# Alternating row halves and column halves of TensorE in the attention stage of a one-layer decoder kernel

## The chip, the cores and the metric

The kernel runs on one core of a Trainium2 chip. The metric is the device time of one execution in microseconds (us); lower is better. All data are f32.

## The reference, cut to what matters

One decoder layer over 256 tokens of width 1024: an RMS norm, a combined input projection, two attention branches beside each other, gates and output projection, and then a sparse feed-forward layer with 32 experts, of which each token takes four. The two branches are what matters here:

```python
# branch A (MLA): 8 heads, keys and queries of 64 + 32 = 96, values of 64, one K and V per head
s = (einsum('bqhd,bkhd->bhqk', qn, k_nope) + einsum('bqhr,bkr->bhqk', qp, k_rot)) * 96 ** -0.5
p = softmax(where(causal, s, -inf));  out_a = einsum('bhqk,bkhd->bqhd', p, v)

# branch B (DSA): an indexer picks 64 keys per query, then 8 query heads share ONE K and ONE V of 64
rel = relu(einsum('bqhd,bkd->bqhk', q_idx, k_idx) * 64 ** -0.5)      # 8 index heads, one index key
score = where(causal, einsum('bqh,bqhk->bqk', w_idx, rel), -inf)
_, sel = top_k(score, 64)
s = einsum('bqhd,bqkd->bhqk', q, k[sel]) * 64 ** -0.5
p = softmax(where(valid, s, -inf));      out_b = einsum('bhqk,bqkd->bqhd', p, v[sel])
```

The kernel doesn't gather: it computes all scores of branch B and adds a mask of the keys that aren't selected.

## The kernel before, in words

Every engine runs its own program, written out by hand, and waits on counting semaphores. There is no planner: the order of the text is the order of each engine's queue. The 256 tokens are two tiles of 128 (`t` = 0, 1). Because of causality a query tile `t` needs only `w = 128 * (t + 1)` keys.

**Front stage.** `raw` is a ring of six slots of 2 MB into which SP (`load_front`, L410) loads the weights in order. `z_unit` (L516) does the input projection in four parts. The index queries are turned (`turn_pairs`, L544) into `qT`, which holds two heads per column block: the even head in rows 0 to 63 and the odd head in rows 64 to 127. `kT` holds the one key twice, in both row halves. Then come the index scores (L589), the turning of branch B's queries, the up projections of branch A (L616), the turning of its queries and keys (L634), and the attention loop (L681). `gate_block` (L558) is a piece of other work, 16 of which compute the gates; the tables `GATES_IDX` and `GATES_ATT` (L61, L62) say after which batches one is put in, to give PE something to do while other engines work. One block is eight matmuls of 256 columns. Then come the branch projections (`branch`, L690), the output projection, and the router.

**Batches.** Heads are worked on in batches that fill one PSUM bank of 512 columns: `BATCHES` (L54) has six for one branch, two for `t` = 0 with four heads and four for `t` = 1 with two heads. All heads of one batch have the same parity, so they lie in the same row half of `qT`. In PSUM, head `h`'s output of a value product goes to partitions `64 * (h % 2)` and on, so all value products of one batch lie in the same column half of the array.

`scores` (L531) writes batch `b` to bank `SB[b % 2]`. In the index stage ACT applies a ReLU from there to `prob` (L954, signal `idx_rl`), and DVE adds the weighted heads up into `score` (L1188, L1190, signal `idx_ac`). ACT's ReLU `b` waits for DVE's sum of batch `b - 2`; PE's batch `b` waits for ReLU `b - 2`.

**Attention loop** (L681), 12 batches, 0 to 5 of branch A and 6 to 11 of branch B. Round `b` on PE: `scores_of(b + 1)`, `values(b - 1)`, a gate block, `turn_probs(b)`. The score products of branch A have 96 rows, those of branch B have 64. DVE's `masked(b)` (L1252) scales and masks the scores and takes the maximum, ACT's `exps` (L992) exponentiates, DVE's `normalised(b)` (L1274, signal `p_ok`) divides; PE's `turn_probs(b)` (L654) waits for `p_ok` and transposes; ACT copies the result to `probT` (L1018, signal `pT_ok`), for which `values(b)` (L662) waits. `masked(b)` waits until `turn_probs(b - 2)` has read the same buffer (`pT_ps`). Between these, DVE works off the top-k selection of branch B (`topk`, L1201) in pieces of three rounds, and the rest of it ahead of `masked(6)`.

```python
            for b in range(12):
                if b < 11:
                    scores_of(b + 1)
                if b:
                    values(b - 1)
                if b in GATES_ATT:
                    gate_block()
                turn_probs(b)
```

**Expert loop** (L885). Per item four `gate_up` and two `down` units of 2 MB each go through the ring; PE, per unit, adds one to `used` and SP loads the next unit into the freed slot (L473). The expert loads before that, the first of them while the front stage still runs, wait for the front units whose slots they take (`used_up`, L348).

In the profile, lines are those of the innermost helper: L493 is `gemm` (gate blocks, up projections, `branch`), L497 a transpose, L535 a score product, L672 a value product, L770 the gather of tokens, L803 the scatter, L835 `gate_up`.

Of the kernel before, what the change touches and what calls it, by code (L numbers as in the profile page):

```python
# [8 lines left out]
ACT = mybir.ActivationFunctionType  # L9
# [5 lines left out]
P = 128  # L15
# [8 lines left out]
Q_LORA, KV_LORA, NOPE, ROPE, V_DIM = 256, 128, 64, 32, 64  # L24
QK = NOPE + ROPE
HD, ROT = 64, 16
# [24 lines left out]

BATCHES = [(0, (0, 2, 4, 6)), (0, (1, 3, 5, 7)),  # L54
           (1, (0, 2)), (1, (1, 3)), (1, (4, 6)), (1, (5, 7))]


WARM = (4, 10, 6, 4)


GATES_IDX = (3,)  # L61
GATES_ATT = (0, 1, 2, 3, 4, 5, 6, 7, 8, 9, 10)  # L62


# [20 lines left out]
def build(nc, x, positions, attn_norm_g, w_in, mla_q_norm_g, mla_w_uq, mla_kv_norm_g, mla_w_ukv,  # L85
# [4 lines left out]
    with ctx:  # L90
# [42 lines left out]
        v_ml = fb("v_ml", [P, TT, HEADS, V_DIM])  # L133
# [61 lines left out]
        B = [ctx.enter_context(nc.psum_tensor(f"bank{i}", [P, BLK], F32)) for i in range(8)]  # L195
        ZB, TB, SB, VB = B[0:2], B[2:4], B[4:6], B[6:8]
        TURN = TB + SB
        ACC, GU, PREP, DN = B[0:4], B[4:6], B[6], B[7]

        def const(name, rows=P):  # L200
# [289 lines left out]
        def _(pe):  # L490
# [5 lines left out]
            def turned(o, src):  # L496
                return pe.transpose(o, src, ident)  # L497
# [30 lines left out]
                    mm.then_inc(z_ps, 1)  # L528
                    z_n += 1

            def scores(b, q, k, signal):  # L531
                t, heads = BATCHES[b % 6]
                w = P * (t + 1)
                for m, h in enumerate(heads):
                    mm = pe.matmul(SB[b % 2][:, m * w:(m + 1) * w], q(h, t), k(h, w), start=True, stop=True)  # L535
                mm.then_inc(signal, 1)

            def pair_q(h, t):
                return qT[HD * (h % 2):HD * (h % 2) + HD, h // 2, t * P:(t + 1) * P]

            def pair_k(h, w):
                return kT[HD * (h % 2):HD * (h % 2) + HD, 0:w]

            def turn_pairs(zq, signal):  # L544

                for j in range(4):
                    for t in range(TT):
                        a = (j % 2) * TOKENS + t * P
                        tr = turned(TB[j // 2][:, a:a + P], zq[:, t, j * P:(j + 1) * P])
                    if j % 2:  # L550
                        tr.then_inc(signal, 1)
                for t in range(TT):
                    tr = turned(VB[0][:, t * P:(t + 1) * P], kk[:, t, :, :].rearrange("p a d -> p (a d)"))
                tr.then_inc(signal, 1)
# [31 lines left out]
            turn_pairs(z_qi, qi_ps)  # L586
            z_unit(3)
            pe.wait_ge(qi_ok, 3)
            for b in range(6):  # L589
                if b >= 2:  # L590
                    pe.wait_ge(idx_rl, b - 1)
                scores(b, pair_q, pair_k, idx_ps)
                if b in GATES_IDX:
                    gate_block()

            pe.wait_ge(qb_rot, 1)
            turn_pairs(z_qb, qd_ps)
            gate_block()

# [46 lines left out]
            def scores_of(b):  # L646
                if b >= 2:
                    pe.wait_ge(s_mx, b - 1)
                if b < 6:
                    scores(b, lambda h, t: qmT[:, h, t * P:(t + 1) * P], lambda h, w: kmT[:, h, 0:w], s_ps)  # L650
                else:
                    scores(b, pair_q, pair_k, s_ps)

            def turn_probs(b):  # L654
                pe.wait_ge(p_ok, b + 1)
                if b >= 2:
                    pe.wait_ge(pT_ok, b - 1)
                for m in range(4):
                    tr = turned(TB[b % 2][:, m * P:(m + 1) * P], prob[:, b % 2, m * P:(m + 1) * P])
                tr.then_inc(pT_ps, 1)  # L660

            def values(b):  # L662
                t, heads = BATCHES[b % 6]
                pe.wait_ge(pT_ok, b + 1)
                if b in (6, 8):
                    pe.wait_ge(pv_ok, t + 1)
                for m in range(4):
                    h = heads[m // (t + 1)]
                    kt = m % (t + 1)
                    half = V_DIM * (h % 2)  # L670
                    v = v_ml[:, kt, h, :] if b < 6 else z_kv[:, kt, HD:2 * HD]
                    mm = pe.matmul(VB[t][half:half + V_DIM, (h // 2) * P:(h // 2 + 1) * P], v,  # L672
                                   probT[:, b % 2, m * P:(m + 1) * P], start=kt == 0, stop=kt == t)
                mm.then_inc(pv_ps, 1)

# [3 lines left out]
            pe.wait_ge(up_a, 8)  # L679
            scores_of(0)  # L680
            for b in range(12):  # L681
                if b < 11:
                    scores_of(b + 1)
                if b:
                    values(b - 1)
                if b in GATES_ATT:
                    gate_block()
                turn_probs(b)
# [8 lines left out]
            pe.wait_ge(pv_ok, 2)  # L697
            pe.wait_ge(s_mx, 12)
            branch(0, 0)
            values(11)  # L700
            branch(0, 1)
            landed_front(pe, U_BR + 1)
            pe.wait_ge(pv_ok, 4)
# [204 lines left out]
        def _(act):  # L908
# [41 lines left out]
            for b in range(6):  # L950
                act.wait_ge(idx_ps, b + 1)
                if b >= 2:
                    act.wait_ge(idx_ac, b - 1)
                act.activation(prob[:, b % 2, :], SB[b % 2][:, :], ACT.Relu, scale=HD ** -0.5).then_inc(idx_rl, 1)  # L954
                if b in GATES_IDX:
                    gate_evac()
            for j in range(2):
                act.wait_ge(qd_ps, j + 1)
# [31 lines left out]
                act.copy(qmT[:, 2 * j:2 * j + 2, :].rearrange("p h t -> p (h t)"), TURN[2 * j % 4][0:QK, :]).then_inc(mq_ok, 1)  # L990

            def exps(b):  # L992
                t, heads = BATCHES[b % 6]
                w = P * (t + 1)
                act.wait_ge(s_mx, b + 1)
                for m in range(len(heads)):
                    ex = act.activation(prob[:, b % 2, m * w:(m + 1) * w], prob[:, b % 2, m * w:(m + 1) * w], ACT.Exp,
                                        bias=mx[:, b % 2, m:m + 1], accum_out=den[:, b % 2, m:m + 1])
                ex.then_inc(p_ex, 1)
# [110 lines left out]
        def _(dve):  # L1110
# [68 lines left out]
            dve.tensor_tensor(rw[:, :, :], rw[:, :, :], g_ffn[:, :].unsqueeze(2).to_broadcast([P, KC, EXPERTS]),  # L1179
                              ALU.mult).then_inc(rw_ok, 1)  # L1180
            for b in range(6):
                t, heads = BATCHES[b]
# [12 lines left out]
                dve.wait_ge(idx_ac, b + 1)  # L1195
# [55 lines left out]

            def masked(b):  # L1252

                t, heads = BATCHES[b % 6]
                w, n = P * (t + 1), len(heads)
                scale = (QK if b < 6 else HD) ** -0.5
                src = SB[b % 2][:, :].rearrange("p (h k) -> p h k", h=n)
                pr = prob[:, b % 2, :].rearrange("p (h k) -> p h k", h=n)
                dve.wait_ge(s_ps, b + 1)
                if b >= 2:  # L1260
                    dve.wait_ge(pT_ps, b - 1)
                if b >= 6:
                    mask = allow[:, t, 0:w].unsqueeze(1).to_broadcast([P, n, w])
                    step(dve.scalar_tensor_tensor(out=pr, in0=src, scalar=scale, in1=mask, op0=ALU.mult, op1=ALU.add))
                else:
                    if t:
                        dve.tensor_scalar(pr[:, :, 0:P], src[:, :, 0:P], scale, None, ALU.mult)
                    mask = const("causal").unsqueeze(1).to_broadcast([P, n, P])
                    step(dve.scalar_tensor_tensor(out=pr[:, :, t * P:w], in0=src[:, :, t * P:w], scalar=scale, in1=mask,
                                                  op0=ALU.mult, op1=ALU.add))  # L1270
                step(dve.tensor_reduce(mx[:, b % 2, 0:n], pr, AXX, ALU.max))
                dve.tensor_scalar(mx[:, b % 2, 0:n], mx[:, b % 2, 0:n], -1.0, None, ALU.mult).then_inc(s_mx, 1)

            def normalised(b):  # L1274
                t, heads = BATCHES[b % 6]
# [243 lines left out]
```

## Time and profile before

| | |
|---|---|
| median of 3 runs | 1183.23 us (1181.96 to 1184.37) |
| the profiled execution | 1181.82 us, span 1180.0 us |
| mean granted TensorE clock | 0.995 |
| PE (matmul) busy | 1102.3 us, 93% |
| PE weight loads | 473.9 us, 40% |
| DVE busy | 279.0 us, 24% |
| ACT busy | 164.0 us, 14% |
| POOL busy | 10.2 us, 1% |
| read from memory | 429.92 MB, 365 GB/s over the span |

The span is what the trace covers, from the first instruction to the last; the execution's own time is 1.82 us longer. Busy shares are averages over stages that differ: the front stage, some 240 us, and the expert loop, the rest. A record `64*128 64x256 f32 x8` is eight records of matmuls that use 64 rows and 128 columns of the array and stream 256 columns of data; a matmul of f32 leaves two records, a transpose one. The records of a matmul are pipelined, so a group's duration overlaps with the start of the next one.

### The profile page before, as it was taken

How to read it: one execution, taken by the hardware profiler on the slowest of the kernel's cores; microseconds unless marked ns; L12 is line 12 of the kernel's file. 1: busy time of each engine (PE TensorE's matmuls, PEld its weight loads, DVE VectorE, ACT ScalarE, POOL GpSimd, SP SyncE). 2: the span in 40 equal slices, each digit the busy share in tenths (PEclk: the TensorE clock that was granted, in tenths of full speed). 3: DMA queues.
4: the chain of work that ended last, by engine and by line, in shares of the span. 5: the costliest groups of instructions: out<-in, count | busy, mean ns of one | idle time of the engine just before them, and what ended most of it. 6: DMA issues, size and time to landing. Idle time of an engine off the chain costs nothing.

```text
span 1180.0 us, 13249 instructions
## 1 busy us (share of the span) xinstructions
PE 1102.3 (93%) x5094; PEld 473.9 (40%) x5094; DVE 279.0 (24%) x662; ACT 164.0 (14%) x341; POOL 10.2 (1%) x28
## 2 busy tenths in 40 slices
PE   7999999999999999999999999999999999999996
PEld 5578887633333333333333333333333333333332
DVE  2056432321111211111111111111111111111113
ACT  2144440210001000000000000000000000000002
POOL 0101000000000000000000000000000000000000
PEclk9999999999999999999999999999999999999998
DMA  9823313469999999999999999999999999999993
GB/s 307 315 75 147 136 72 126 160 288 405 429 429 430 427 427 430 429 428 427 429 429 429 427 427 430 429 428 427 429 429 430 427 427 430 429 428 427 429 429 158
DMA packets 43265, 431.22 MB, mean 365 GB/s; under 512 B 5808, under 2 KB 7984, under 8 KB 18640
## 3 DMA queue, kind: packets, MB, share of 16 engines
q1 hardware_dynamic: 42960, 430.46, 87.2%
q10 hardware_dynamic: 288, 0.52, 0.1%
q8 instruction: 11, 0.18, 0.1%
q14 instruction: 6, 0.05, 0.0%
HBM read 429.92 MB, written 1.05 MB: 365 GB/s over the span
## 4 chain that ended last, share of the span: by engine, by line
DMA 57%; PE 41%; DVE 1%; issue 1%; ACT 1%; SPq 0%; DVEq 0%; ACTq 0%
DMA raw<-in_w_gate_up 56%; PE bank L835 15%; PE bank L493 8%; PE bank L526 4%; PE bank L851 4%; PE bank L718 2%; PE bank L497 2%; PE bank L535 1%; PE bank L672 1%; PE bank L770 1%; PE bank L803 1%; DMA x_res<-in_x 1%; PE bank L736 0%; PE bank L813 0%; DVE x_res L1457 0%
## 5 line engine op out<-in xcount | busy, mean ns | idle before, releaser
L835 PE MATMUL bank<-raw,xT 128*64 128x512 f32 x2048 | 465.2, 598 | 56.0 <-DMA raw<-in_w_gate_up 54.4
L835 PEld LDWEIGHTS bank<-raw,xT 128*64 128x64 f32 x2048 | 137.9, 136 | 357.7 <-issue 230.7
L851 PE MATMUL bank<-raw,actT 128*64 128x512 f32 x1024 | 233.2, 597 | 0.0
L1408 DVE COPY ev_gu<-bank 128x512 f32<-128x512 f32 x32 | 22.1, 692 | 532.7 <-PE bank L835 532.7
L851 PEld LDWEIGHTS bank<-raw,actT 128*64 128x64 f32 x1024 | 71.7, 137 | 132.5 <-issue 126.7
L1401 DVE TENSOR_TENSOR gub<-bank,bias_gu 128x512 f32<-128x512 f32 x64 | 43.9, 686 | 169.5 <-PE bank L497 169.5
L1065 ACT COPY ev_gu<-bank 128x512 f32<-128x512 f32 x32 | 18.8, 586 | 413.3 <-PE bank L835 413.3
L803 PE MATMUL bank<-ev_dn,scat 64*128 64x512 f32 x256 | 64.3, 621 | 1.2 <-ACT ev_dn L1075 0.8
L770 PE MATMUL bank<-x_res,onehot 128*64 128x512 f32 x264 | 62.3, 592 | 0.0
L493 PE MATMUL bank<-hT,raw 128*128 128x256 f32 x256 | 58.9, 383 | 0.0
L493 PEld LDWEIGHTS bank<-hT,raw 128*128 128x128 f32 x256 | 47.5, 190 | 8.4 <-issue 2.5
L526 PE MATMUL bank<-raw,hT 128*128 128x512 f32 (+2 forms) x128 | 46.4, 525 | 1.1 <-DVE hT L1142 1.1
L497 PEld LDWEIGHTS bank<-cst,ev_gu 128*128 128x128 f32 x256 | 33.4, 211 | 25.9 <-issue 25.9
L1070 ACT ACTIVATE sig<-gub 128x512 f32<-128x512 f32 x32 | 20.1, 629 | 154.7 <-DVE gub L1410 154.7
L497 PE MATMUL bank<-cst,ev_gu 128*128 128x128 f32 x256 | 39.5, 297 | 0.0
L803 PEld LDWEIGHTS bank<-ev_dn,scat 64*128 64x128 f32 x256 | 22.1, 186 | 41.7 <-issue 41.0
L770 PEld LDWEIGHTS bank<-x_res,onehot 128*64 128x64 f32 x264 | 19.0, 137 | 37.2 <-issue 37.0
L526 PEld LDWEIGHTS bank<-raw,hT 128*128 128x128 f32 x128 | 25.1, 202 | 20.5 <-issue 20.4
L1075 ACT COPY ev_dn<-bank 128x512 f32<-128x512 f32 x32 | 18.8, 586 | 83.1 <-PE bank L851 83.1
L1060 ACT COPY scat<-bank 128x256 f32<-128x256 f32 x32 | 11.9, 372 | 126.7 <-PE bank L497 126.7
L1051 ACT COPY ev_x<-bank 128x512 f32<-128x512 f32 x33 | 19.3, 586 | 66.5 <-PE bank L770 66.5
L1424 DVE TENSOR_TENSOR actT<-gub,sig 128x512 f32<-128x512 f32 x32 | 22.2, 692 | 24.5 <-PE bank L851 24.5
(234 smaller groups left out, 594.1 us busy)
## 6 DMA issues: line engine op xcount, KB each, us to landing
raw<-in_w_gate_up SPq DMA_DIRECT2D x128, 2048.0 KB, 25.4
raw<-in_w_down SPq DMA_DIRECT2D x64, 2048.0 KB, 24.9
raw<-in_w_in SPq DMA_DIRECT2D x6, 2048.0 KB, 14.5
raw<-in_w_out SPq DMA_DIRECT2D x2, 2048.0 KB, 9.7
raw<-in_w_branch_mla SPq DMA_DIRECT2D x1, 2048.0 KB, 9.0
raw<-in_w_branch_dsa SPq DMA_DIRECT2D x1, 2048.0 KB, 7.8
raw<-in_w_in SPq DMA_DIRECT2D x1, 1664.0 KB, 16.8
x_res<-in_x SPq DMA_DIRECT2D x2, 512.0 KB, 4.9
```

Source lines behind the costliest of these rows:

```text
L493: mm = pe.matmul(o, lhs(c), rhs(c), start=start and c == 0, stop=c == n - 1)
L497: return pe.transpose(o, src, ident)
L526: mm = pe.matmul(ZB[t][:, 0:w], hT[:, c, t * P:(t + 1) * P], unit3(n, w)[:, c, :], start=c == 0, stop=c == KC - 1)
L718: mm = pe.matmul(B[2 * t + n][:, :], mT[:, c, t * P:(t + 1) * P], unit3(U_WO + n)[:, c, :], start=c == 0, stop=c == KC - 1)
L770: mm = pe.matmul(PREP[half * SLOTS:(half + 1) * SLOTS, :], onehot[:, t, :], xs[:, t, half * BLK:(half + 1) * BLK], start=t == 0, stop=t == ...
L803: mm = pe.matmul(ACC[2 * t + half][:, :], scat[rows, t * P:(t + 1) * P], ev_dn[rows, :], start=False, stop=True, skip_group_check=True)
L835: mm = pe.matmul(GU[pair][half * SLOTS:(half + 1) * SLOTS, :], xT[:, c, b, :], w[:, at:at + BLK], start=u == 0 and k == 0, stop=last and k ...
L851: mm = pe.matmul(DN[half * SLOTS:(half + 1) * SLOTS, :], actT[:, c, u, :], w[:, at:at + BLK], start=u == 0 and c == 0, stop=u == DN_UNITS ...
L1070: act.activation(sig[:, :], glu, ACT.Sigmoid, scale=ALPHA).then_inc(sig2_ok, 1)
L1401: dve.tensor_tensor(gub[:, pair, :].rearrange("p (j s) -> p j s", s=SLOTS), GU[pair][:, :].rearrange("p (j s) -> p j s", s=SLOTS), bias_gu ...
L1408: dve.tensor_copy(ev_gu[:, 1, :], GU[1][:, :]).then_inc(lin_ev, 1)
L1424: dve.tensor_tensor(actT[:, :, :, :].rearrange("p c h s -> p (c h s)"), lin, sig[:, :], ALU.mult).then_inc(act_ok, 1)
```

## The change

The score products with 64 rows (index scores and branch B's scores) are issued in pairs of batches, the even head in the upper and the odd head in the lower rows in turn, each into its own bank. `PAIR_BATCHES` is the old table. The index scores use `SB`, `TB` and `SB` again, and their gate block comes after batches 2 and 3. Branch A's batches hold neighbouring heads now, so that its 64-wide value products alternate between the column halves; their order is by key tile first. Branch B's value products have the same V for all heads, so each half's product streams all heads of the batch at once (512 columns for `t` = 0, 256 for `t` = 1), and `turn_probs` puts the transposed blocks in that order for `b >= 8`. In the loop, branch B's scores come at `b` = 5, 7 and 9, its value products at `b` = 8 and 10 and after the loop.

```diff
-BATCHES = [(0, (0, 2, 4, 6)), (0, (1, 3, 5, 7)),
-           (1, (0, 2)), (1, (1, 3)), (1, (4, 6)), (1, (5, 7))]
+BATCHES = [(0, (0, 1, 2, 3)), (0, (4, 5, 6, 7)),
+           (1, (0, 1)), (1, (2, 3)), (1, (4, 5)), (1, (6, 7))]
+PAIR_BATCHES = [(0, (0, 2, 4, 6)), (0, (1, 3, 5, 7)),
+                (1, (0, 2)), (1, (1, 3)), (1, (4, 6)), (1, (5, 7))]
-GATES_IDX = (3,)
+GATES_IDX = (2,)
+        IDX_BANKS = (SB, TB, SB)
...
+            def pair_scores(b, banks, signal):
+                t = PAIR_BATCHES[b][0]
+                w, n = P * (t + 1), len(PAIR_BATCHES[b][1])
+                for m in range(n):
+                    for k in range(2):
+                        h = PAIR_BATCHES[b + k][1][m]
+                        rows = slice(HD * k, HD * k + HD)
+                        mm = pe.matmul(banks[k][:, m * w:(m + 1) * w], qT[rows, h // 2, t * P:(t + 1) * P], kT[rows, 0:w],
+                                       start=True, stop=True)
+                        if m == n - 1:
+                            mm.then_inc(signal, 1)
...
-            for b in range(6):
-                if b >= 2:
-                    pe.wait_ge(idx_rl, b - 1)
-                scores(b, pair_q, pair_k, idx_ps)
+            for b in range(0, 6, 2):
+                if b == 4:
+                    pe.wait_ge(idx_rl, 2)
+                pair_scores(b, IDX_BANKS[b // 2], idx_ps)
                 if b in GATES_IDX:
                     gate_block()
             pe.wait_ge(qb_rot, 1)
+            pe.wait_ge(idx_rl, 4)
             turn_pairs(z_qb, qd_ps)
...
                 if b < 6:
-                    scores(b, lambda h, t: qmT[:, h, t * P:(t + 1) * P], lambda h, w: kmT[:, h, 0:w], s_ps)
+                    scores(b)
                 else:
-                    scores(b, pair_q, pair_k, s_ps)
+                    pe.wait_ge(s_mx, b)
+                    pair_scores(b - 6, SB, s_ps)
...
-                    tr = turned(TB[b % 2][:, m * P:(m + 1) * P], prob[:, b % 2, m * P:(m + 1) * P])
+                    at = (m % 2) * 2 + m // 2 if b >= 8 else m
+                    tr = turned(TB[b % 2][:, at * P:(at + 1) * P], prob[:, b % 2, m * P:(m + 1) * P])
...
             def values(b):
-                t, heads = BATCHES[b % 6]
+                t, heads = BATCHES[b]
                 pe.wait_ge(pT_ok, b + 1)
-                if b in (6, 8):
-                    pe.wait_ge(pv_ok, t + 1)
-                for m in range(4):
-                    h = heads[m // (t + 1)]
-                    kt = m % (t + 1)
-                    half = V_DIM * (h % 2)
-                    v = v_ml[:, kt, h, :] if b < 6 else z_kv[:, kt, HD:2 * HD]
-                    mm = pe.matmul(VB[t][half:half + V_DIM, (h // 2) * P:(h // 2 + 1) * P], v,
-                                   probT[:, b % 2, m * P:(m + 1) * P], start=kt == 0, stop=kt == t)
+                for kt in range(t + 1):
+                    for n, h in enumerate(heads):
+                        m = n * (t + 1) + kt
+                        half = V_DIM * (h % 2)
+                        mm = pe.matmul(VB[t][half:half + V_DIM, (h // 2) * P:(h // 2 + 1) * P], v_ml[:, kt, h, :],
+                                       probT[:, b % 2, m * P:(m + 1) * P], start=kt == 0, stop=kt == t)
                 mm.then_inc(pv_ps, 1)
+            def pair_values(b):
+                t, heads = PAIR_BATCHES[b - 6]
+                pe.wait_ge(pT_ok, b + 2)
+                pe.wait_ge(pv_ok, t + 1)
+                n = len(heads) * P
+                at = (heads[0] // 2) * P
+                for kt in range(t + 1):
+                    for k in range(2):
+                        mm = pe.matmul(VB[t][V_DIM * k:V_DIM * (k + 1), at:at + n], z_kv[:, kt, HD:2 * HD],
+                                       probT[:, (b + k) % 2, kt * n:(kt + 1) * n], start=kt == 0, stop=kt == t)
+                        if kt == t:
+                            mm.then_inc(pv_ps, 1)
...
             for b in range(12):
-                if b < 11:
+                if b < 6 or b in (7, 9):
                     scores_of(b + 1)
-                if b:
+                if 0 < b < 7:
                     values(b - 1)
+                elif b in (8, 10):
+                    pair_values(b - 2)
                 if b in GATES_ATT:
                     gate_block()
                 turn_probs(b)
...
             branch(0, 0)
-            values(11)
+            pair_values(10)
             branch(0, 1)
```

ACT's ReLU reads from `IDX_BANKS` and evacuates the index stage's gate block after batch 3; ACT's and DVE's loops take their heads from the table that PE uses. Their instructions are the same in number and size.

## Rows read from the trace of the kernel before

**Rows 1.** The page's 40 equal slices (29.5 us each): PE busy, granted clock, memory rate.

```profile
PE   7999999999999999999999999999999999999996
PEclk9999999999999999999999999999999999999998
GB/s 307 315 75 147 136 72 126 160 288 405 429 429 430 427 427 430 429 428 427 429 429 429 427 427 430 429 428 427 429 429 430 427 427 430 429 428 427 429 429 158
```

**Rows 2.** Timeline of the SP queue, 0 to 250 us: start, length, what.

```profile
140.19 107.54 SPq L435 DMA_DIRECT2D raw<-in_w_gate_up  x8
```

**Rows 3.** Timeline of PE at the index scores (second row: a window of the first part).

```profile
61.32 3.52 PE L535 MATMUL bank<-kT,qT 64*128 64x128 f32 x24
...
61.32 1.71 PE L535 MATMUL bank<-kT,qT 64*128 64x128 f32 x16
...
64.77 3.72 PE L493 MATMUL bank<-hT,raw 128*128 128x256 f32 x16
68.42 1.14 PE L535 MATMUL bank<-kT,qT 64*128 64x256 f32 x8
69.50 1.09 PE L497 MATMUL bank<-cst,z_qb 128*128 128x128 f32 x8
```

**Rows 4.** The chain that ended last, at the index scores: start, length, what.

```profile
62.51 0.60 ACT area_p L954
...
63.16 1.68 PE bank L535 x8
```

**Rows 5.** Timeline of PE in the attention loop, b=6 (first two rows) and b=7.

```profile
134.34 1.16 PE L535 MATMUL bank<-kT,qT 64*128 64x128 f32 x8
135.42 1.09 PE L672 MATMUL bank<-area_p,v_ml 128*64 128x128 f32 x8
...
140.00 0.60 PE L497 MATMUL bank<-cst,area_p 128*128 128x128 f32 x4
140.53 1.13 PE L535 MATMUL bank<-kT,qT 64*128 64x256 f32 x4
141.58 1.09 PE L672 MATMUL bank<-area_p,z_kv 128*64 128x128 f32 x8
142.60 3.72 PE L493 MATMUL bank<-hT,raw 128*128 128x256 f32 x16
146.16 0.60 PE L497 MATMUL bank<-cst,area_p 128*128 128x128 f32 x4
```

**Rows 6.** Timeline of PE around one gather (L770) and one scatter (L803).

```profile
254.06 1.89 PE L770 MATMUL bank<-x_res,onehot 128*64 128x512 f32 x8
255.88 0.69 PE L813 MATMUL bank<-gain,gateT 32*128 32x512 f32 x1
...
294.39 1.99 PE L803 MATMUL bank<-ev_dn,scat 64*128 64x512 f32 x8
296.31 1.08 PE L835 MATMUL bank<-raw,xT 128*64 128x512 f32 x4
```

**Rows 7.** Timeline of PE: the transposes of `turn_probs(2)` and `turn_probs(3)`.

```profile
115.67 0.60 PE L497 MATMUL bank<-cst,area_p 128*128 128x128 f32 x4
...
121.65 0.60 PE L497 MATMUL bank<-cst,area_p 128*128 128x128 f32 x4
```

**Rows 8.** Timeline of DVE: the last instruction of `normalised(2)` and `normalised(3)`.

```profile
113.60 0.69 DVE L1280 TENSOR_TENSOR area_p<-area_p,den 128x512 f32<-128x512 f32 x1
...
120.62 0.69 DVE L1280 TENSOR_TENSOR area_p<-area_p,den 128x512 f32<-128x512 f32 x1
```

**Rows 9.** Busy us (instructions) in a stretch: PE, weight loads, DVE, ACT, POOL; clock, DMA.

```profile
112.00:118.00 6.00, 6.00 (x34) 4.95 (x32) 5.69 (x17) 2.52 (x7) 0.00 (x0) 1.00 0.13 34
```

**Rows 10.** Timeline of PE from `turn_probs(10)` to the branch projection; in brackets idle time.

```profile
164.65 0.60 PE L497 MATMUL bank<-cst,area_p 128*128 128x128 f32 x4
165.92 1.09 PE L672 MATMUL bank<-area_p,z_kv 128*64 128x128 f32 x8 [0.68 <-ACT area_p L1018]
...
170.27 1.99 PE L493 MATMUL bank<-q_ml,raw 128*128 128x256 f32 x8
```

More of the change, by code:

```diff
@@ L529, in z_unit, with scores @@
                     z_n += 1
-            def scores(b, q, k, signal):
-                t, heads = BATCHES[b % 6]
+            def scores(b):
+                t, heads = BATCHES[b]
                 w = P * (t + 1)
                 for m, h in enumerate(heads):
[L535 to L542, printed above, removed]
+                    mm = pe.matmul(SB[b % 2][:, m * w:(m + 1) * w], qmT[:, h, t * P:(t + 1) * P], kmT[:, h, 0:w],
+                                   start=True, stop=True)
+                mm.then_inc(s_ps, 1)
+            def pair_scores(b, banks, signal):
[6 more added lines that the diff above has]
+                        mm = pe.matmul(banks[k][:, m * w:(m + 1) * w], qT[rows, h // 2, t * P:(t + 1) * P], kT[rows, 0:w],
+                                       start=True, stop=True)
+                        if m == n - 1:
+                            mm.then_inc(signal, 1)
             def turn_pairs(zq, signal):
@@ L658, in turn_probs @@
                 for m in range(4):
-                    tr = turned(TB[b % 2][:, m * P:(m + 1) * P], prob[:, b % 2, m * P:(m + 1) * P])
+                    at = (m % 2) * 2 + m // 2 if b >= 8 else m
+                    tr = turned(TB[b % 2][:, at * P:(at + 1) * P], prob[:, b % 2, m * P:(m + 1) * P])
                 tr.then_inc(pT_ps, 1)
             def values(b):
-                t, heads = BATCHES[b % 6]
+                t, heads = BATCHES[b]
                 pe.wait_ge(pT_ok, b + 1)
-                if b in (6, 8):
-                    pe.wait_ge(pv_ok, t + 1)
-                for m in range(4):
-                    h = heads[m // (t + 1)]
-                    kt = m % (t + 1)
-                    half = V_DIM * (h % 2)
-                    v = v_ml[:, kt, h, :] if b < 6 else z_kv[:, kt, HD:2 * HD]
-                    mm = pe.matmul(VB[t][half:half + V_DIM, (h // 2) * P:(h // 2 + 1) * P], v,
-                                   probT[:, b % 2, m * P:(m + 1) * P], start=kt == 0, stop=kt == t)
-                mm.then_inc(pv_ps, 1)
+                for kt in range(t + 1):
[4 more added lines that the diff above has]
+                                       probT[:, b % 2, m * P:(m + 1) * P], start=kt == 0, stop=kt == t)
+                mm.then_inc(pv_ps, 1)
+            def pair_values(b):
[10 more added lines that the diff above has]
+                            mm.then_inc(pv_ps, 1)
             pe.wait_ge(up_d, 4)
@@ L953, in _ @@
                     act.wait_ge(idx_ac, b - 1)
-                act.activation(prob[:, b % 2, :], SB[b % 2][:, :], ACT.Relu, scale=HD ** -0.5).then_inc(idx_rl, 1)
-                if b in GATES_IDX:
+                act.activation(prob[:, b % 2, :], IDX_BANKS[b // 2][b % 2][:, :], ACT.Relu, scale=HD ** -0.5).then_inc(idx_rl, 1)
+                if b - 1 in GATES_IDX:
                     gate_evac()
@@ L992, in exps @@
             def exps(b):
-                t, heads = BATCHES[b % 6]
+                t, heads = (BATCHES + PAIR_BATCHES)[b]
                 w = P * (t + 1)
@@ L1181, in _ @@
             for b in range(6):
-                t, heads = BATCHES[b]
+                t, heads = PAIR_BATCHES[b]
                 w = P * (t + 1)
@@ L1252, in masked @@
             def masked(b):
-                t, heads = BATCHES[b % 6]
+                t, heads = (BATCHES + PAIR_BATCHES)[b]
                 w, n = P * (t + 1), len(heads)
@@ L1274, in normalised @@
             def normalised(b):
-                t, heads = BATCHES[b % 6]
+                t, heads = (BATCHES + PAIR_BATCHES)[b]
                 w, n = P * (t + 1), len(heads)
```

## The prediction

> **What bounds the kernel now.** I read the page's slices first [rows 1]. From the eleventh slice on (295 us) the memory delivers 427 to 430 GB/s until the last: the expert loop runs at the rate of its weight loads. In slices three to eight it delivers 72 to 160 while PE is at nine tenths or more: there PE is what everything waits for. The SP queue [rows 2] shows how the two stages meet: its first eight loads of expert weights run from 140.19 to 247.73, each issued when PE has freed a ring slot, the last two when the first `gate_up` calls have used theirs. The stream of loads can therefore start no earlier than PE reaches the experts, and from there its length is bytes over rate. So a microsecond taken off PE's chain before the experts is a microsecond off the end, and one given to an engine that isn't in that chain is nothing.
>
> Then the front stage on PE in order of time. An f32 matmul stands in the trace as two records, so the 16 index score matmuls are 32 records. In the rows of a timeline the start of a group to the start of the next is what the group costs; its own duration includes a tail that overlaps the next.
>
> **Index scores: 1.5 us.** [rows 3] The first four batches take 61.32 to 64.77, 3.45 us. Inside is a wait: batch 2 starts at 63.16 only when ACT has read bank 0 of `SB` [rows 4]. The last two batches, four records each with 256 columns, take 68.42 to 69.50, 1.08 us. A single batch of four such records in the second branch takes 1.05 us [rows 5]. So batches 4 and 5, one in the upper and one in the lower rows, already run wholly beside each other although the program lists them one after the other. Batches 0 and 1 overlap in part: 16 records from 61.32, 1.71 us long, where 8 records of the same shape alone are 1.16 long [rows 3, 5].
> Here a page contradicts the row. The Trainium skill ("TensorE: Matmul & The Clock Gate", What overlaps and what doesn't) says that matmuls keep program order and only weight loads are pulled ahead. By that rule batches 4 and 5 would now cost 1.9 us, the change would win another 0.85 us there, and the whole sum would be 8.7 us. The row decides: the win there is nothing.
> After the change the first pair is eight slots in both halves at once, 1.08 us as the 8 records of one batch [rows 5], the second pair 1.08 us as the last pair now [rows 3]; between them no change of array shape and, since the second pair writes `TB`, no wait on ACT. A shape change costs about 0.2: 8 records at 0.11 would be 0.88 of the 1.08. So 2.16 - 0.2 = 1.96 instead of 3.45: **1.5 us**. The third pair comes a gate block later, stays at 1.08, and finds bank 0 and 1 long read. The new wait for four ReLUs ahead of `turn_pairs`, at about 68.0, costs nothing: `scores(5)` waits for the same four today and finds them done at 68.4 with no idle time [rows 3], and what they hang on, DVE's sums of batches 0 and 1, starts as now (bound: 0 to 0.4 us). DVE and ACT see the last pair 1.5 us earlier too, so what PE needs from them later (the latents, the evacuations of the up projections) moves along.
>
> **First branch, value products: 1.6 us of a possible 2.6.** The scores there have 96 rows; only their heads change, not their cost. A `values` call is 8 records of 128 columns, 1.02 us [rows 5], of which 0.2 to change shape and the rest 0.11 a record. Does alternating short products between column halves halve that? No row has it at 128 columns. Lower bound of the gain: nothing. Upper: the 512-column rows, where 8 records in alternating column halves take 1.82 us [rows 6], 0.22 each; that is what a record of 256 columns takes in one place (16 in a gate block of 3.56 us [rows 5]), an exact half. The nearest in width are the row halves at 128 columns, whose loads and products overlap fully [rows 3]. I take the half: 1.02 becomes 0.59, 0.43 less per call.
> But three of six calls stand ahead of a wait. DVE works through the top-k rounds with no gap (5.69 of 6 us busy [rows 9], the rest its steps between instructions) and its rate doesn't depend on PE here. `turn_probs(b)` needs `normalised(b)`. For b=2 that ends at 114.29 and PE comes at 115.67; for b=3 it ends at 121.31 and PE comes at 121.65 [rows 7, 8]; for b=1 the slack is more than one call's gain. With `values(0)`, (1), (2) 0.43 shorter each, PE would be at `turn_probs(2)` at 114.81, still behind DVE, but at `turn_probs(3)` at 120.36 and waits until 121.36. Of 1.29 us only 0.29 stays; DVE is late next. `values(3)`, (4) and (5) count in full, 1.29. Together **1.58**.
>
> **Second branch, scores: 3.2 us.** Six batches become three calls of two. By the index row a pair costs what one batch costs [rows 3, 5]. What goes: one 128-column batch (134.34 to 135.42, 1.08) and two of 256 columns (1.05 each): **3.2 us**. Lower bound 0.6, if only the shape changes go.
>
> **Second branch, value products: 3.1 us.** Now six calls of 1.02 (141.58 to 142.60) [rows 5] = 6.1. After, at t=0 two matmuls of 512 columns, one per half, four records in two slots; at t=1 four matmuls of 256 columns, eight records in four slots. Two slots of 512 columns are 0.86 us plus some 0.15 for the shape change, by the 1.82 for four [rows 6], and four of 256 the same: 1.0 a call, 3.0 in all: **3.1 us**. If the halves didn't overlap a call would be about 1.9, and 0.4 us would be left (lower bound).
>
> **Waits that lose their cover: 1.5 us back.** `values(b-1)` needs ACT's copy of the turned probabilities. Now `scores_of(b+1)` runs in between and hides it; for the last b there is nothing between: from the transposes at 164.65 to `values(10)` at 165.92 is 1.27 us, with a stall of 0.68 on ACT's copy, against 140.00 to 140.53 = 0.53 where PE just goes on [rows 5, 10]. After the change this happens at b=6, 8 and 10, and no longer at b=11: (3 - 1) x 0.74 = **1.5 us** lost. At b=11 `turn_probs(11)` follows `turn_probs(10)` at once; its probabilities are ready, since scores 10 and 11 were both made at b=9. The last `pair_values` stands behind `branch(0, 0)` as `values(11)` does now, eight records of 256 columns or 1.8 us, which cover two copies that are each shorter than the stall of 0.68 [rows 10].
> Do DVE and ACT still keep up? The odd batch of a pair is masked only after the transposes of the batch before last (`pT_ps`): `masked` is two passes and `normalised` one over 512 columns, 0.69 each [rows 8], with small steps an estimated 2.5 us, against a wait or score call of about 1 us and the gate block of 3.56 us that PE does meanwhile [rows 5]. Slack about 1 us or more in every round, nothing lost; without the gate block some 2 us a round would be. The waits on `s_mx` for both banks are met by what `turn_probs` has already waited for.
>
> **Sum.** 1.5 + 1.6 + 3.2 + 3.1 - 1.5 = 7.9 us. The profiled execution took 1181.82 us (span 1180.0, 1.8 around it), 1.4 below the median 1183.23. So 1173.9 for a like execution and **1175.3 us** against the median. A measurement can tell about 0.2% (2.4 us) from no change.
>
> **Rivals.**
> *Narrow products don't pair as well* (chance 0.2). If short value products gain nothing, 1.6 us go; if in addition each uncovered wait is 1.3 rather than 0.74, another 1.1: 5.2 us won, 1178.0. For it: at 128 columns two streams need four instructions in 0.11 us. Against it: the index rows do that already.
> *The front isn't what starts the stream, or DVE and ACT take the win* (0.07). Then 1182 to 1183.5. For it: six ring slots are loaded ahead of the loop. Against: PE's row of the page is full in the front and SP's loads follow PE [rows 1, 2].
> *Slower: each change of half drains the array* (0.03). 66 matmuls would alternate (16 index, 16 scores, 24 and 10 values). At 0.2 us, the price of a change of shape, that is 13 us; a drain also rules out any overlap, so the gains go and the waits of 1.5 stay: 1183.2 + 13 + 1.5 = 1198. Counted against the forecast alone it decides from (7.9 + 2.4) / 66 = 0.16 us per change. Against it: the gather alternates column halves at 1.82 us for 8 records, the scatter row halves at 1.92 [rows 6], no room for a drain at each. The Trainium skill ("TensorEngine Tiling (Array Packing)", Key Properties) also says that a change of mode drains the engine and a change of tile doesn't; the trace agrees.
> *A larger win* (0.05): the wait at `turn_probs(3)` doesn't appear, 8.9 us, 1174.3.
>
> **How the numbers follow.** The forecast has 0.65. Its own range is 1175.3 with the runs' spread of 1.2 either side and the terms' errors, 1173 to 1177.5. To hold 8 in 10 the range takes in most of the first rival: 1172.3 to 1179.3. Faster by over 0.2% (below 1180.9) holds for forecast, first rival and larger win: 0.90; within 0.2% 0.07; slower 0.03.
>
> **What would show it.** In the profile after: index scores of the first two pairs as one group of about 2.0 us with no ACT wait, a gate block from 63.3; a group of 8 records at 256 columns costing 1.05 in the second branch; `values` groups 0.6 apart; a DVE wait of about 1 us at the fourth `turn_probs` and three waits of 0.7 on ACT's copy; the block of the branch projection that now starts at 170.27 [rows 10] at 162.3; the loop unchanged. Wrong would be: records in the two halves that start 0.1 us or more apart, waits of PE on `normalised` other than at b=3, or an expert loop whose length changed.

## The result, and the profile after

| | before | after |
|---|---|---|
| median | 1183.23 us (1180.44 to 1187.07, 7 runs) | 1177.81 us (1171.85 to 1178.35, 7 runs) |
| ratio after to before | | 0.9936, 95% interval 0.9911 to 0.9962 |
| the profiled execution | 1181.82 us, span 1180.0 | 1171.85 us, span 1170.1 |

The change makes the kernel faster: the ratio is that of the two means, 1176.2 and 1183.8 us, so 0.64% or 7.5 us, with an interval of 4.5 to 10.5 us. The two medians differ by 5.4 us and the two profiled executions by 10.0, against a forecast of 7.9. Single executions of one kernel differ by several us in parts that the change doesn't touch (below), so the step by step comparison goes by one stretch that both traces have: from the first index score to the second block of the branch projection. It took 61.32 to 170.27 = 108.95 us before [rows 3, 10].

The timeline of PE after the change, at the index scores (start, length, line, matmul, records):

```profile
59.00 2.03 PE L552 MATMUL bank<-kT,qT 64*128 64x128 f32 x24
60.95 3.72 PE L498 MATMUL bank<-hT,raw 128*128 128x256 f32 x16
64.61 1.13 PE L552 MATMUL bank<-kT,qT 64*128 64x256 f32 x8
65.67 1.09 PE L502 MATMUL bank<-cst,z_qb 128*128 128x128 f32 x8
```

The first four batches cost 1.95 us for 3.45, the last two 1.06 for 1.08 [rows 3]. The wait on the ReLU [rows 4] is gone, and the new wait for four ReLUs doesn't appear. The same timeline in the attention loop, with idle time in brackets:

```profile
112.39 0.66 PE L685 MATMUL bank<-area_p,v_ml 128*64 128x128 f32 x8
112.98 3.72 PE L498 MATMUL bank<-hT,raw 128*128 128x256 f32 x16
117.56 0.66 PE L502 MATMUL bank<-cst,area_p 128*128 128x128 f32 x4 [0.86 <-DVE area_p L1309]
...
123.69 1.16 PE L552 MATMUL bank<-kT,qT 64*128 64x128 f32 x16
124.78 0.66 PE L685 MATMUL bank<-area_p,v_ml 128*64 128x128 f32 x8
...
128.93 0.60 PE L502 MATMUL bank<-cst,area_p 128*128 128x128 f32 x4
130.20 0.66 PE L685 MATMUL bank<-area_p,v_ml 128*64 128x128 f32 x8 [0.68 <-ACT area_p L1047]
130.79 3.72 PE L498 MATMUL bank<-hT,raw 128*128 128x256 f32 x16
134.35 0.60 PE L502 MATMUL bank<-cst,area_p 128*128 128x128 f32 x4
134.88 1.14 PE L552 MATMUL bank<-kT,qT 64*128 64x256 f32 x8
135.94 3.72 PE L498 MATMUL bank<-hT,raw 128*128 128x256 f32 x16
139.50 0.60 PE L502 MATMUL bank<-cst,area_p 128*128 128x128 f32 x4
140.77 1.08 PE L698 MATMUL bank<-area_p,z_kv 128*64 128x512 f32 x4 [0.68 <-ACT area_p L1047]
141.78 3.72 PE L498 MATMUL bank<-hT,raw 128*128 128x256 f32 x16
...
160.05 1.99 PE L498 MATMUL bank<-q_ml,raw 128*128 128x256 f32 x8
```

A `values` call of the first branch is 0.59 (112.39 to 112.98) for 1.02 [rows 5]. Sixteen score records of a pair take 1.09 (123.69 to 124.78), what eight took [rows 5]; eight of 256 columns take 1.06, what four took. A `pair_values` call is 1.01. PE waits 0.86 us for DVE at the fourth `turn_probs`, and 0.68 on ACT's copy in rounds 6 and 8, and once more in round 10. The stretch is 59.00 to 160.05 = **101.05 us, 7.90 less than before**; the forecast's sum was 7.9. PE reaches the first `gate_up` 10.2 us earlier than before (7.9 from the stretch and 2.3 because the index scores happened to start at 59.00 and not at 61.32), and the execution ends 10.0 us earlier: what PE saves ahead of the experts arrives at the end.

### The profile page after: what moved, and what is told of

Same layout as the page of the kernel before. It is cut to its first block, busy times and chain, and to the rows that moved or that the text cites. A ratio compares the mean times of both kernels' runs of the same rounds, so it can differ in the third digit from the quotient of the medians.

```text
span 1170.1 us, 13198 instructions
## 1 busy us (share of the span) xinstructions
PE 1091.0 (93%) x5066; PEld 462.4 (40%) x5066; DVE 279.2 (24%) x662; ACT 163.5 (14%) x341; POOL 10.2 (1%) x28
## 4 chain that ended last, share of the span: by engine, by line
DMA 57%; PE 39%; DVE 2%; ACT 1%; issue 1%; SPq 0%; DVEq 0%; ACTq 0%
DMA raw<-in_w_gate_up 57%; PE bank L864 15%; PE bank L498 7%; PE bank L531 4%; PE bank L880 4%; PE bank L747 2%; PE bank L502 2%; PE bank L832 1%; PE bank L799 1%; PE bank L552 1%; PE bank L765 0%; DMA x_res<-in_x 0%; PE bank L842 0%; DVE work L1238 0%; DVE top L1236 0%
## 5 line engine op out<-in xcount | busy, mean ns | idle before, releaser
L880 PEld LDWEIGHTS bank<-raw,actT 128*64 128x64 f32 x1024 | 71.6, 137 | 132.0 <-issue 126.2
```

The costliest lines, as they stand in the source:

```text
L880: mm = pe.matmul(DN[half * SLOTS:(half + 1) * SLOTS, :], actT[:, c, u, :], w[:, at:at + BLK], start=u == 0 and c == 0, stop=u == DN_UNITS ...
```

## The experiments

Each is an edit of the changed kernel, and each is read by its stretch in one trace. The first six kernels below ran only once each, so their whole times say little; `both`, `after_again` and the two after them ran six times.

**The index stage put back** (`old_index`; scores in program order through `SB` alone, gate block after batch 3):

```diff
-            for b in range(0, 6, 2):
-                if b == 4:
-                    pe.wait_ge(idx_rl, 2)
-                pair_scores(b, IDX_BANKS[b // 2], idx_ps)
+            for b in range(6):
+                if b >= 2:
+                    pe.wait_ge(idx_rl, b - 1)
...
+                    mm = pe.matmul(SB[b % 2][:, m * w:(m + 1) * w], qT[rows, h // 2, t * P:(t + 1) * P], kT[rows, 0:w],
+                                   start=True, stop=True)
```

> The changed kernel with its index stage put back (six batches in the old order, one per ReLU wait, gate block after batch 3). Measure: the stretch from the first index score to the second block of the branch projection, 108.95 us before and 101.05 after the change. My theory: the index pairing is worth 1.5 us, all of it in the first four batches (a wait on ACT and part of the overlap), so 102.55; the last two batches cost 1.08 as in both kernels. The rival from the page (matmuls keep program order, so batches 4 and 5 ran one after the other before) would want 2.35, so 103.4, with 1.9 us for the last two batches.

Measured: 62.50 to 165.05 = 102.55. PE's timeline of this run at the index scores:

```profile
62.50 3.52 PE L609 MATMUL bank<-kT,qT 64*128 64x128 f32 x24
65.96 3.72 PE L498 MATMUL bank<-hT,raw 128*128 128x256 f32 x16
69.61 1.14 PE L609 MATMUL bank<-kT,qT 64*128 64x256 f32 x8
70.68 1.09 PE L502 MATMUL bank<-cst,z_qb 128*128 128x128 f32 x8
```

Putting the index stage back costs 1.50 us, in the first four batches (3.46). The last two, listed one after the other, take 1.07: they gain nothing.

**Where the first branch's saving counts** (`first_two`, `last_four`; the second also loops over heads outside of key tiles):

```diff
-BATCHES = [(0, (0, 1, 2, 3)), (0, (4, 5, 6, 7)),
+BATCHES = [(0, (0, 2, 4, 6)), (0, (1, 3, 5, 7)),
            (1, (0, 1)), (1, (2, 3)), (1, (4, 5)), (1, (6, 7))]
```

```diff
 BATCHES = [(0, (0, 1, 2, 3)), (0, (4, 5, 6, 7)),
-           (1, (0, 1)), (1, (2, 3)), (1, (4, 5)), (1, (6, 7))]
+           (1, (0, 2)), (1, (1, 3)), (1, (4, 6)), (1, (5, 7))]
```

> The changed kernel with the first two batches of the first branch put back to heads of one parity, so that values(0) and values(1) lie in one column half each. My theory: each of the two calls costs 0.43 us more (1.02 for 0.59), but they stand ahead of the wait for DVE at the fourth turn_probs, 0.86 us in the changed kernel, which shrinks to nothing: the stretch stays at 101.05 to 101.2. The rival (every saved us on PE counts) wants 101.9.

> The changed kernel with the last four batches of the first branch put back to heads of one parity. My theory: values(2) is absorbed by the wait for DVE, values(3), (4) and (5) count 0.43 us each: 101.05 + 1.3 = 102.35. The rival (every saved us counts) wants 102.8; if the narrow value products didn't gain, nothing would move.

Measured: `first_two` 62.37 to 163.42 = 101.06 us (from times not rounded), `last_four` 59.64 to 161.99 = 102.35. The same edit, 0.43 us a call, costs 0.01 us in two calls and 1.30 in four. In `last_four` `values(2)` is longer again and only shortens the wait for DVE, from 0.86 to 0.44 us; the next three calls count:

```profile
113.04 1.09 PE L685 MATMUL bank<-area_p,v_ml 128*64 128x128 f32 x8
...
118.22 0.66 PE L502 MATMUL bank<-cst,area_p 128*128 128x128 f32 x4 [0.44 <-DVE area_p L1309]
...
119.67 1.09 PE L685 MATMUL bank<-area_p,v_ml 128*64 128x128 f32 x8
120.68 3.72 PE L498 MATMUL bank<-hT,raw 128*128 128x256 f32 x16
```

In `first_two` PE comes to the fourth `turn_probs` with no idle time; the row has no bracket:

```profile
116.62 0.66 PE L685 MATMUL bank<-area_p,v_ml 128*64 128x128 f32 x8
117.21 3.72 PE L498 MATMUL bank<-hT,raw 128*128 128x256 f32 x16
120.94 0.66 PE L502 MATMUL bank<-cst,area_p 128*128 128x128 f32 x4
```

So DVE sets the time of that point (with its top-k, as `both` below shows), and what PE saves ahead of it is lost but for the slack it had.

**Is the alternation itself needed?** (`grouped`; in each pair all products of one half come first):

```diff
-                for m in range(n):
-                    for k in range(2):
+                for k in range(2):
+                    for m in range(n):
...
-                    for n, h in enumerate(heads):
+                    for n, h in sorted(enumerate(heads), key=lambda x: x[1] % 2):
```

> The changed kernel, but inside every pair all products of the one half are issued before those of the other (row halves for scores, column halves for the first branch's values). My theory from the trace of before: PE lets products of the other half pass by about four matmuls ahead, so pairs of 256 columns (2 + 2 matmuls) still cost 1.06, and pairs of 128 columns (4 + 4 matmuls) about 1.6 instead of 1.1, twice: 101.05 + 1.0 = 102.1, if column halves behave as row halves. The rival (program order is kept, the page's rule) makes every grouped pair serial: at least 0.9 us more per pair of scores and 0.4 per call of values that counts, 107 or more.

Measured: 61.13 to 163.30 = 102.17. Timeline of its PE, at the index scores, at a 128-column pair and at a 256-column pair of the second branch:

```profile
61.13 2.58 PE L552 MATMUL bank<-kT,qT 64*128 64x128 f32 x24
...
126.38 1.71 PE L552 MATMUL bank<-kT,qT 64*128 64x128 f32 x16
128.02 0.66 PE L685 MATMUL bank<-area_p,v_ml 128*64 128x128 f32 x8
...
138.11 1.14 PE L552 MATMUL bank<-kT,qT 64*128 64x256 f32 x8
139.19 1.99 PE L498 MATMUL bank<-hT,raw 128*128 128x256 f32 x8
```

Two matmuls of one half, then two of the other (256 columns) cost 1.08, for 1.06 in turn. Four and four (128 columns) cost 1.64 for 1.09 in the second branch, and the first four index batches take 2.51 (61.13 to 63.64) for 1.95; in series four and four would be, by my estimate, 16 slots of 0.11 and 0.2, some 2.0. The column halves do the same: a `values` call with two and two matmuls is 0.59. So matmuls of a free half pass those that wait in front of them, but only a few. The starts of the single records in this trace say how few: with four and four, the second half's first record starts 0.55 us after the first half's, when three of the first half's eight records have still to start; with two and two it starts 0.013 us after, again with three to go. The same run splits the 1.50 us of the index stage. With the new banks, and so without the waits on the ReLU, the first four batches go from 3.46 to 2.51; taking the halves in turn brings them from 2.51 to 1.95.

**Half or width?** (`narrow_values`; `pair_values` one head at a time, 128 columns, still alternating):

```diff
-                for kt in range(t + 1):
-                    for k in range(2):
-                        mm = pe.matmul(VB[t][V_DIM * k:V_DIM * (k + 1), at:at + n], z_kv[:, kt, HD:2 * HD],
-                                       probT[:, (b + k) % 2, kt * n:(kt + 1) * n], start=kt == 0, stop=kt == t)
+                for n in range(len(heads)):
+                    for kt in range(t + 1):
+                        for k in range(2):
...
+                            mm = pe.matmul(VB[t][V_DIM * k:V_DIM * (k + 1), (h // 2) * P:(h // 2 + 1) * P], z_kv[:, kt, HD:2 * HD],
+                                           probT[:, (b + k) % 2, m * P:(m + 1) * P], start=kt == 0, stop=kt == t)
```

> The changed kernel with the second branch's value products one head at a time (128 columns each), still alternating between the column halves. My theory: what made the 3.1 us is the halves, not the wider stream: a call is 8 slots of 0.11 us and 0.2 for the change of shape, 1.07 instead of 1.02, so the stretch is 101.05 + 3 x 0.06 = 101.2. The rival (the wide stream does it, by fewer weight loads) gives 1.9 to 2.0 a call as if unpaired: 103.8.

Measured: 101.07. The sixteen records of a call take 1.02 us (162.92 to 163.94):

```profile
162.92 1.09 PE L699 MATMUL bank<-area_p,z_kv 128*64 128x128 f32 x16
163.94 1.99 PE L498 MATMUL bank<-q_ml,raw 128*128 128x256 f32 x8
```

The wide stream over all heads brings 0.02 us. The 3.1 us come from issuing two calls as one with their halves in turn. No run has merged calls in one half; by the prediction's own bound for that case (about 1.9 us a call), some 0.4 of the 3.1 is the merging and the rest the halves.

**Covering the new waits** (`gate_first`), **and the wait for DVE too** (`both`):

```diff
+                if b in (6, 8, 10):
+                    gate_block()
                 if 0 < b < 7:
                     values(b - 1)
                 elif b in (8, 10):
                     pair_values(b - 2)
-                if b in GATES_ATT:
+                if b in GATES_ATT and b not in (6, 8, 10):
                     gate_block()
```

```diff
-                        if r % 3 == 2:
+                        if r % 3 == 2 or (t and r == TOPK // 8 - 1):
                             yield
```

> The changed kernel with the gate block ahead of the value products in rounds 6, 8 and 10, where the products wait for ACT's copy. My theory: the three waits of 0.68 us are all that the lost cover costs, and DVE and ACT have more than 1 us of slack in these rounds: each round is 0.75 to 0.8 shorter, the stretch 98.75. The rival (the waits only move, to turn_probs waiting for normalised) keeps 101.0.

> The gate block first in rounds 6, 8 and 10, and DVE's top-k cut once more, so that its last piece (about 3.2 us of selection after the eight rounds) comes after normalised(3) instead of before masked(4). My theory: the wait of 0.86 us at the fourth turn_probs goes too, 1.0 with what stands around it: stretch 97.7, and a time 3.3 us under the changed kernel's. The rival (DVE is late one round later instead, at turn_probs(4), where it has 1.5 us) would keep 98.75.

> The changed kernel itself, beside the others on one chip. The stretch is 101.05 again to 0.1 us. What differs between runs lies outside: before the index scores (59.0 to 62.5 us so far) and from the loop to the end (939.8 or 942.5), and goes with the granted clock at the start and at 220 to 265 us.

Measured: `gate_first` 98.68, `both` 97.60, `after_again` 101.05. PE's timeline of `gate_first` in round 8, no idle time left:

```profile
142.52 0.60 PE L502 MATMUL bank<-cst,area_p 128*128 128x128 f32 x4
142.96 3.62 PE L498 MATMUL bank<-hT,raw 128*128 128x256 f32 x16
146.51 1.08 PE L698 MATMUL bank<-area_p,z_kv 128*64 128x512 f32 x4
147.52 0.66 PE L502 MATMUL bank<-cst,area_p 128*128 128x128 f32 x4
```

The three waits were worth 2.37 us and the wait for DVE 1.08; DVE isn't late elsewhere. In `both` the fourth `turn_probs` has no idle time in front of it:

```profile
115.08 3.72 PE L498 MATMUL bank<-hT,raw 128*128 128x256 f32 x16
118.64 0.60 PE L502 MATMUL bank<-cst,area_p 128*128 128x128 f32 x4
```

In this comparison the kernel before had a median of 1185.16 us, `after_again` 1177.0 (ratio 0.9935, interval 0.9917 to 0.9954) and `both` **1172.15** (ratio 0.9899, interval 0.9879 to 0.9919). The means of `both` and `after_again`, 1172.5 and 1176.7 us, differ by 4.2 us, nearly four times its standard error of 1.1 (an estimate from the spread of the six runs of each). So `both` beats both kernels, the changed one by 4.9 us of median, of which the stretch explains 3.45.

**What makes runs of one kernel differ.** The changed kernel's runs span 1171.85 to 1178.35, more than any term of the sum, though the stretch is 101.05 in both of its traces. Outside it three times vary. They belong to parts that, but for the two kernels at the end of this section, are the same in all kernels here, so all 12 traces can be laid side by side:

| part | times, us (traces) | granted clock |
|---|---|---|
| start to index scores | 59.0 to 59.6 (3) | 1.00 at 12 to 16 us |
| | 60.5 to 61.3 (5) | 0.57 to 0.62 at 12 to 16 us |
| | 62.4 to 62.9 (4) | no record before 17.7 us |
| end of the stretch to first `gate_up` | 70.0 (9) | 1.00 at 218 to 234 us |
| | 71.6 (3) | 0.89 at 218 to 234 us |
| first `gate_up` to the end | 939.3 to 940.1 (7) | 0.89 to 1.00 at 250 to 266 us |
| | 942.4 to 942.5 (4) | 0.79 at 250 to 266 us |
| | 941.6 (1, `both_warm2`) | 0.98 at 250 to 266 us |

Windows of the changed kernel's first run (busy us and records of each engine; behind them the granted clock, DMA share, GB/s):

```profile
12.00:16.00 4.00, 4.00 (x24) 3.62 (x23) 3.71 (x17) 0.00 (x0) 0.00 (x0) 1.00 1.10 323
...
246.00:254.00 8.00, 6.48 (x28) 3.38 (x28) 3.72 (x7) 2.26 (x3) 0.00 (x0) 1.00 1.00 426
254.00:262.00 8.00, 8.00 (x40) 3.13 (x37) 0.85 (x3) 0.00 (x0) 0.00 (x0) 1.00 0.88 330
```

and of `narrow_values`, whose index scores started at 62.87 and whose last part took 942.5; its first `gate_up` comes 3.9 us later, so its last two windows are 4 us later too:

```profile
12.00:16.00 4.00, 3.46 (x10) 3.49 (x11) 3.93 (x14) 0.00 (x0) 0.00 (x0) 1.00 1.10 340
16.00:20.00 4.00, 4.00 (x19) 4.00 (x19) 1.82 (x10) 0.58 (x2) 0.00 (x0) 1.00 1.06 283
250.00:258.00 8.00, 6.57 (x22) 3.56 (x22) 3.23 (x6) 2.17 (x3) 0.00 (x0) 0.73 1.00 428
258.00:266.00 8.00, 8.00 (x34) 2.79 (x32) 1.44 (x4) 0.00 (x0) 0.00 (x0) 0.84 0.58 201
```

At 258 to 266 us the granted clock is 0.84, part of the time at 1.2 GHz, where the fast run has 1.00 at the same point of its loop; PE does 34 records for 40, and DMA moves 201 GB/s for 330. In the first stretch PE does 10 matmul records for 24. This trace has no record of the clock before 18.2 us, and the window then prints 1.00, so there the rate of records, not the column, suggests the lower level. The longer times thus go with the lower clock, except that a mean of 0.89 at 250 to 266 us (`after_again`) still goes with 939.3. Two more kernels tried to remove this, `both` with nine matmuls of a zeroed tile before x has landed (`both_warm`), and with eight more in the idle time after the first expert's products (`both_warm2`):

```diff
+            pe.wait_ge(warm_ok, 1)
+            for _ in range(9):
+                pe.matmul(B[7][:, 0:P], area_p[:, 0:P], area_p[:, P:2 * P], start=True, stop=True)
...
             turn_tokens(1)
+            for _ in range(8):
+                pe.matmul(DN[:, 0:P], const("ones"), ident, start=True, stop=True)
```

> The faster version (gate block first, top-k cut once more) with nine matmuls of a zeroed tile ahead of the first transposes, while PE waits for x. My theory of the spread between runs of one kernel: the granted clock is at 1.2 GHz until 8 to 18 us and falls again for some us between 220 and 265 in some runs; the attention stretch isn't part of it. Then the clock is at its full level before the first input projection in every run, the index scores start by 59.0 us or earlier instead of 59.0 to 62.9, and the median falls by 1 to 3 us from 1172.15; the spread of the loop's part stays. The rival (the start is late because x and the first weights land late) keeps the start of the index scores between 59 and 63.

> As the last, with eight more matmuls into a free bank in the 2.5 us in which PE waits for the second expert's tokens. My theory: the loop's second length (942.4 instead of 939.3 to 940.1) comes from a clock of 1.2 GHz at 253 to 263 us, after the idle time there, and doesn't occur. If the fall has nothing to do with that idle time, both lengths still occur, or the loop is up to 1 us longer by the added work.

Measured: `both_warm` 1171.44 (1168.14 to 1173.94; ratio to before 0.9906, interval 0.9884 to 0.9928), `both_warm2` 1171.67 (1170.72 to 1173.88; 0.991, interval 0.989 to 0.993). That is no difference from `both` (0.9899) that these runs can tell. In `both_warm` the granted clock is 1.00 at 12 to 16 us and the index scores started at 59.35; in `both_warm2`, with the same nine matmuls, it is 0.62 and they started at 60.47. The eight matmuls of `both_warm2` did fill the idle time, and the clock fell all the same. Windows of `both_warm2`, then of `both`:

```profile
246.00:262.00 16.00, 16.00 (x78) 8.30 (x78) 4.67 (x9) 0.63 (x1) 0.00 (x0) 0.89 0.83 332
...
248.00:250.00 2.00, 2.00 (x11) 2.00 (x11) 0.80 (x2) 0.00 (x0) 0.00 (x0) 0.50 1.09 467
250.00:252.00 2.00, 0.83 (x4) 0.43 (x3) 1.45 (x3) 0.63 (x1) 0.00 (x0) 0.69 1.01 434
```

In `both_warm2` PE was busy for all of the 16 us, and the clock was 0.89. In `both` it was at 1.2 GHz (0.50) from 248 to 250 us, while PE was busy, and PE's idle time came only behind that, from 250.8 on. In `narrow_values`, of the slower kind, the order is the same: 0.50 from 254 us on, idle from 255.7 on. Just before the fall PE had done products of 32 rows (244.31 to 248.00 in `both`), with transposes behind them. So the theory that the clock falls after the idle time is wrong in these traces: it falls ahead of it. The part from the first `gate_up` to the end took 941.6 us, against 939.4 in `both_warm`; the added matmuls explain at most 1 of these 2.2 us by what was expected, and the rest stays open. The remedy failed; that the clock goes with the spread is seen in the profiles, but what makes it fall and how to hold it are left open.

## Why the prediction was right

Point by point, in the profile after:

| step | forecast | measured |
|---|---|---|
| index scores | 1.5 | 1.50 (`old_index`) |
| first branch's values | 1.58: 0.29 ahead of the wait, 1.29 behind it | 1.02 to 0.59 a call; ahead of the wait 0.27, behind it 1.30 (`last_four`) |
| wait for DVE at the fourth `turn_probs` | about 1.0 | 0.86 idle, worth 1.08 (`both`) |
| second branch's scores | 3.2 | 3.2: pairs at 1.09 and 1.06, the price of one batch |
| second branch's values | 3.1 | 3.1: 1.01 a call for two of 1.02 |
| waits on ACT's copy | three for one, 1.5 lost | three, 0.68 each; all three with what stands around them 2.37 (`gate_first`) |
| stretch in all | 7.9 | 7.90 |
| loop | unchanged | 939.8 before, 940.0 after, in the two first profiles |

The 0.27 is from `scores(0)` to the fourth `turn_probs`: 98.22 to 121.65 before, 94.40 to 117.56 after. The terms were right one by one, so the sum isn't luck: 1.50 + 1.57 + 3.2 + 3.1 less the 1.5 of two more waits is 7.9.

The measured 1177.81 is 2.5 us above the forecast of 1175.3 and inside the range; the ratio gives 7.5 us for the change. The missing 2.5 us are not in the stretch. They are the spread described above: the median of before came from three runs at first, and of the changed kernel's seven runs five lie at 1176.7 to 1178.4 and two at 1171.9 and 1172.7. My range took in 1.2 us for the runs' spread, from three runs; that was the term of it that was too small.

The rival of narrow products that don't pair fell with the 0.59, the one of drains with the trace: 66 changes of half and no gap, and in the pair at 123.69 the records of the two halves start under 0.01 us apart, where 0.1 would have been a sign of being wrong. The rival of a larger win fell with the 0.86 us wait, which was there. That the front doesn't start the stream fell with the end, 10.0 us earlier for 10.2 at the loop. The gate block that the prediction puts at 63.3 and the branch projection at 162.3 came 2.3 us sooner (60.95 and 160.05), all of it the earlier start of the index scores.

The rule of the Trainium skill that matmuls keep program order ("TensorE: Matmul & The Clock Gate", What overlaps and what doesn't) would have made the last two index batches of `old_index` cost 1.9 us if they ran wholly in series. Strict order is a little weaker than that: the second half's first record may start beside the first half's last, which by my estimate from the slots is 1.7 us for these two batches and 1.85 for four and four matmuls of 128 columns. They cost 1.07 and, in `grouped`, 1.64, and three records of the first half start after the second half's first. The measurement decides against the rule as it stands.

## What to carry to other kernels

Products of 64 rows or 64 output columns cost about half here when the two halves work beside each other, the rows at 128 and 256 columns, the output columns from 128 to 512; lay out the heads so that neighbours in the queue use different halves, and don't bother to widen the stream. Before counting a saving on the engine that bounds the stage, find the next point at which it waits for another one: here 1.29 us saved ahead of it were worth 0.27, the slack that there was, and 1.29 behind it all of it. When two calls are merged, look at what the removed call was hiding; putting other work there got back 2.4 us for one moved line, and cutting one piece of DVE's work in two another 1.1.

## What I had not expected of the hardware

The spread between runs, some 6 us, is larger than any term of the sum and lies in three places that the change doesn't touch. The longer times go with a lower granted clock: 0.79 at 250 to 266 us in the four traces with the long last part. It fell while PE was busy (0.50 at 248 to 250 us in `both`, with 2.00 of 2 us busy), and nine added matmuls from 1.2 us on didn't bring the index scores forward reliably (59.35 and 60.47 us, against 59.00 to 62.87 without). And the reach of the overlap: a half that is free starts its products ahead of three waiting records of the other. So two matmuls of 256 columns in one half are passed completely by two of the other, four of 128 columns only in part.
